# HGRN output products split into score and state parts, chunk-state and inverse products in turn over row groups

## What is computed

```python
# HGRN2, per head and chunk of 64 tokens (q, k, v: tokens x 128)
inter  = (q * exp(b)) @ S                       # what the state gives
scores = sum_k q[t,k] * k[s,k] * exp(b[t,k] - b[s,k]), s <= t
o      = inter + scores @ v
S      = exp(b_end) * S + (k * exp(b_end - b)).T @ v

# gated delta rule: per head and chunk T = inverse(I + A), A strictly lower triangular 64 x 64
```

## Time and profile before

| | |
|---|---|
| Runs, median of 3 | 2732.92 us (2729.94 to 2734.82) |
| Profiled execution, span from first to last instruction | 2725.5 us |
| its own time outside of the span | not recorded; the median of the runs is 7.4 us above the span |
| Mean granted TensorE clock | 0.995 of 2.4 GHz |
| Busy: TensorE, its weight loads, VectorE, ScalarE, GpSimd | 98%, 65%, 46%, 24%, 2% |
| Load of a 2 MB weight block, issue to landing, median | 7.8 us |

### The profile page before, as it was taken

How to read it: one execution, slowest core, us unless ns; L and a number is a source line. 1 busy time by engine, 2 the same in 40 slices (tenths; PEclk the granted TensorE clock), 3 DMA queues, 4 the chain that set the end, 5 groups by cost and what they waited for, 6 DMA issues and landing times.

```text
span 2725.5 us, 28695 instructions
## 1 busy us (share of the span) xinstructions
PE 2672.6 (98%) x11362; PEld 1773.7 (65%) x11362; DVE 1259.9 (46%) x2490; ACT 658.4 (24%) x1491; POOL 60.1 (2%) x116
## 2 busy tenths in 40 slices
PE   8999999999999999999999999999999999999999
PEld 4445557656478888746556664655555684788886
DVE  5733333444334456425363426465564451344564
ACT  2122331246200000222342123525252202000001
POOL 0000000000000000000000001011010000000000
PEclk9999999999999999999999999999999999999999
DMA  4211012100122222120110131121120411222222
GB/s 156 76 48 62 31 64 82 61 32 10 66 80 93 93 93 70 69 93 32 62 62 32 64 124 55 39 78 47 62 76 34 177 62 62 92 93 93 81 74 78
DMA packets 120445, 194.88 MB, mean 71 GB/s; under 512 B 5148, under 2 KB 61272, under 8 KB 119416
## 3 DMA queue, kind: packets, MB, share of 16 engines
q1 hardware_dynamic: 118848, 180.82, 19.6%
q0 software_dynamic: 1344, 12.19, 1.2%
q10 hardware_dynamic: 120, 0.03, 0.0%
HBM read 185.69 MB, written 7.34 MB: 71 GB/s over the span
## 4 chain that ended last, share of the span: by engine, by line
PE 96%; ACT 2%; DVE 1%; issue 1%; DMA 0%; ACTq 0%; DVEq 0%
PE psum L532 20%; PE psum L529 15%; PE psum L2312 14%; PE psum L418 9%; PE psum L2294 8%; PE psum L403 6%; PE psum L438 5%; PE psum L1165 2%; PE psum L2162 2%; PE psum L455 2%; PE psum L1185 2%; PE psum L462 1%; PE psum L1173 1%; PE psum L660 1%; PE psum L391 1%
## 5 line engine op out<-in xcount | busy, mean ns | idle before, releaser
L2312 PE MATMUL psum<-weight_ring,h_t 128*128 128x512 f32 x896 | 409.0, 600 | 3.1 <-ACT arena L2593 1.9
L585 DVE TENSOR_TENSOR arena<-arena,psum 128x512 f32<-128x512 f32 x179 | 122.9, 687 | 346.7 <-PE psum L532 287.6
L2312 PEld LDWEIGHTS psum<-weight_ring,h_t 128*128 128x128 f32 x896 | 163.3, 192 | 165.8 <-issue 162.4
L418 PE MATMUL psum<-h_t,weight_ring 128*128 128x512 f32 x544 | 235.6, 594 | 2.2 <-DVEq L3032 0.8
L2294 PE MATMUL psum<-h_t,weight_ring 128*128 128x512 f32 x512 | 233.0, 598 | 0.9 <-DVE arena L2912 0.9
L532 PE MATMUL psum<-h_t,weight_ring 128*128 128x256 f32 x1024 | 228.2, 380 | 0.0
L529 PE MATMUL psum<-weight_ring,arena 128*128 128x256 f32 x992 | 222.2, 382 | 2.3 <-ACT arena L2722 1.5
L532 PEld LDWEIGHTS psum<-h_t,weight_ring 128*128 128x128 f32 x1024 | 194.9, 190 | 27.1 <-issue 1.3
L529 PEld LDWEIGHTS psum<-weight_ring,arena 128*128 128x128 f32 x992 | 189.9, 192 | 28.8 <-issue 3.3
L418 PEld LDWEIGHTS psum<-h_t,weight_ring 128*128 128x128 f32 x544 | 102.9, 190 | 130.9 <-issue 128.9
L403 PE MATMUL psum<-weight_ring,h_t 128*128 128x512 f32 (+1 forms) x384 | 162.3, 580 | 0.8 <-DVEq L1640 0.8
(11 more groups left out here) (409 smaller groups left out, 3407.6 us busy)
## 6 DMA issues: line engine op xcount, KB each, us to landing
weight_ring<-in_ffn_w_in_dram SPq DMA_DIRECT2D x44, 1024.0 KB, 6.8
weight_ring<-in_w_in_dram SPq DMA_DIRECT2D x20, 2048.0 KB, 7.8
weight_ring<-in_ffn_w_out_dram SPq DMA_DIRECT2D x8, 2048.0 KB, 7.9
weight_ring<-in_w_in_even_dram SPq DMA_DIRECT2D x7, 2048.0 KB, 8.2
weight_ring<-in_w_in_odd_dram SPq DMA_DIRECT2D x5, 2048.0 KB, 7.8
weight_ring<-in_w_in_dram SPq DMA_DIRECT2D x8, 1024.0 KB, 7.0
weight_ring<-in_w_branch_gdn_dram SPq DMA_DIRECT2D x4, 2048.0 KB, 7.8
weight_ring<-in_ffn_w_out_dram SPq DMA_DIRECT2D x4, 1536.0 KB, 6.9
```

The source lines that it names most:

```text
L418: last = pe.matmul(bank, slot[:, k, c:c + P], act[:, k, :], start=(k == 0), stop=(k == KD - 1))
L585: ins = dve.tensor_tensor(out, other, bank, op)
L2312: last = pe.matmul(bank, act[:, k, t * P:(t + 1) * P], slot[:, k, :], start=(k == 0), stop=(k == KD - 1))
```

## The change

In `pe_hgrn_states` the chunk-state products alternate between the two row halves with every product instead of filling one bank and then the other. The outputs are split: the score products of all four tiles go first, into banks of their own (`hd`), ahead of the wait for the states; then the state products of all four tiles, into four banks `ho`, which no longer accumulate. ScalarE copies `hd`, scaled, to `V["o"]`; VectorE adds `ho`, scaled, to it, and ScalarE's squares wait for that. In `pe_gdn_inverse_and_state` the `x5` products alternate between the two halves, and `t5`, `r5` of half 1 and `r5` of half 0 take turns unit by unit.

```diff
--- before.py
+++ after.py
@@ -2259,24 +2259,29 @@
         pe.wait_ge(K.free_of((s, "ke", g, h)), K.turn((s, "ke", g, h)))
         if h == 3:
             pe_take(fill, KD)
-        for par in range(2):
-            p = CH * par
-            bank = pe_fresh(K, pe, (s, "hu", g, h, par))
-            for j in range(NT):
-                last = pe.matmul(bank[:, j * P:(j + 1) * P], V["k"][p:p + CH, h, j * P:(j + 1) * P],
-                                 V["v"][p:p + CH, j, h * P:(h + 1) * P], start=True, stop=True)
-            last.then_inc(K.full_of((s, "hu", g, h, par)), 1)
+        banks = [pe_fresh(K, pe, (s, "hu", g, h, par)) for par in range(2)]
+        for j in range(NT):
+            for par in range(2):
+                p = CH * par
+                ins = pe.matmul(banks[par][:, j * P:(j + 1) * P], V["k"][p:p + CH, h, j * P:(j + 1) * P],
+                                V["v"][p:p + CH, j, h * P:(h + 1) * P], start=True, stop=True)
+                if j == NT - 1:
+                    ins.then_inc(K.full_of((s, "hu", g, h, par)), 1)
     pe_take(fill, KD)
+    for j in range(NT):
+        bank = pe_fresh(K, pe, (s, "hd", g, j))
+        for h in range(4):
+            last = pe.matmul(bank[:, h * P:(h + 1) * P], V["s_t"][:, h * NT + j, :], V["v"][:, j, h * P:(h + 1) * P],
+                             start=True, stop=True)
+        last.then_inc(K.full_of((s, "hd", g, j)), 1)
     pe.wait_ge(K.hgrn_states, g + 1)
     for j in range(NT):
         bank = pe_fresh(K, pe, (s, "ho", g, j))
         for h in range(4):
-            o = bank[:, h * P:(h + 1) * P]
-            last = pe.matmul(o, V["s_t"][:, h * NT + j, :], V["v"][:, j, h * P:(h + 1) * P], start=True, stop=False)
             for c in (2 * j, 2 * j + 1):
                 p = CH * (c % 2)
-                last = pe.matmul(o[p:p + CH, :], V["w"][:, 0, h * T + c * CH:h * T + (c + 1) * CH],
-                                 V["state"][:, h * NC + c, :], start=False, stop=True)
+                last = pe.matmul(bank[p:p + CH, h * P:(h + 1) * P], V["w"][:, 0, h * T + c * CH:h * T + (c + 1) * CH],
+                                 V["state"][:, h * NC + c, :], start=True, stop=True)
         last.then_inc(K.full_of((s, "ho", g, j)), 1)
     K.banks_in_turn = ALL_BANKS
 
@@ -2420,27 +2425,29 @@
     lower, rr, tt, x5, x6 = V["lower"], V["rr"], V["tt"], V["x5"], V["x6"]
     units = range(4 * NT)
     pe.wait_ge(K.blocks_solved, 2 * g + 1)
-    for p in range(2):
-        bank = pe_fresh(K, pe, (s, "x5", g, p))
-        a, b = slice(64 * p, 64 * p + 32), slice(64 * p + 32, 64 * p + 64)
-        for u in units:
-            last = pe.matmul(bank[b, 32 * u:32 * u + 32], lower[a, u, b], V["block"][a, u, :], start=True, stop=True)
-        last.then_inc(K.full_of((s, "x5", g, p)), 1)
+    banks = [pe_fresh(K, pe, (s, "x5", g, p)) for p in range(2)]
+    for u in units:
+        for p in range(2):
+            a, b = slice(64 * p, 64 * p + 32), slice(64 * p + 32, 64 * p + 64)
+            ins = pe.matmul(banks[p][b, 32 * u:32 * u + 32], lower[a, u, b], V["block"][a, u, :], start=True, stop=True)
+            if u == units[-1]:
+                ins.then_inc(K.full_of((s, "x5", g, p)), 1)
     pe_take(fill, 4)
     pe.wait_ge(K.blocks_solved, 2 * g + 2)
     for p in range(2):
         pe.wait_ge(K.free_of((s, "x5", g, p)), K.turn((s, "x5", g, p)))
     b = slice(32, 64)
-    bank = pe_fresh(K, pe, (s, "t5", g))
+    turned = pe_fresh(K, pe, (s, "t5", g))
+    banks = [pe_fresh(K, pe, (s, "r5", g, p)) for p in range(2)]
     for u in units:
-        last = pe.matmul(bank[b, 32 * u:32 * u + 32], V["block_t"][b, u, :], x5[b, u, :], start=True, stop=True)
-    last.then_inc(K.full_of((s, "t5", g)), 1)
-    for p in range(2):
-        a, b = slice(64 * p, 64 * p + 32), slice(64 * p + 32, 64 * p + 64)
-        bank = pe_fresh(K, pe, (s, "r5", g, p))
-        for u in units:
-            last = pe.matmul(bank[a, 32 * u:32 * u + 32], x5[b, u, :], V["block_t"][b, u, :], start=True, stop=True)
-        last.then_inc(K.full_of((s, "r5", g, p)), 1)
+        ins = pe.matmul(turned[b, 32 * u:32 * u + 32], V["block_t"][b, u, :], x5[b, u, :], start=True, stop=True)
+        if u == units[-1]:
+            ins.then_inc(K.full_of((s, "t5", g)), 1)
+        for p in (1, 0):
+            a, c = slice(64 * p, 64 * p + 32), slice(64 * p + 32, 64 * p + 64)
+            ins = pe.matmul(banks[p][a, 32 * u:32 * u + 32], x5[c, u, :], V["block_t"][c, u, :], start=True, stop=True)
+            if u == units[-1]:
+                ins.then_inc(K.full_of((s, "r5", g, p)), 1)
     pe_take(fill, 4)
     pe.wait_ge(K.blocks_placed, 6 * g + 2)
     pe.wait_ge(K.free_of((s, "t5", g)), K.turn((s, "t5", g)))
@@ -2575,9 +2582,11 @@
         else:
             act_gate(K, act, V["gate_y"], (s, "gate_h", 0), 0)
         for j in range(NT):
+            act.wait_ge(K.full_of((s, "hd", g, j)), K.turn((s, "hd", g, j)))
+            act.activation(V["o"][:, j, g * 512:(g + 1) * 512], K.bank((s, "hd", g, j)), ACT.Copy,
+                           scale=DK ** -0.5).then_inc(K.free_of((s, "hd", g, j)), 1)
+        for j in range(NT):
             dst = V["o"][:, j, g * 512:(g + 1) * 512]
-            act.wait_ge(K.full_of((s, "ho", g, j)), K.turn((s, "ho", g, j)))
-            act.activation(dst, K.bank((s, "ho", g, j)), ACT.Copy, scale=DK ** -0.5).then_inc(K.free_of((s, "ho", g, j)), 1)
             act.wait_ge(K.free_of((s, "ho", g, j)), K.turn((s, "ho", g, j)))
             for h in range(4):
                 n = j * 4 + h
@@ -2959,6 +2968,12 @@
                         key = (s, "hu", g, h, c % 2)
                         dve.wait_ge(K.free_of(key), K.turn(key))
         dve.tensor_copy(K.stat[:, 76:77], K.stat[:, 77:78]).then_inc(K.hgrn_states, 1)
+        for j in range(NT):
+            o = V["o"][:, j, g * 512:(g + 1) * 512]
+            dve.wait_ge(K.free_of((s, "hd", g, j)), K.turn((s, "hd", g, j)))
+            dve.wait_ge(K.full_of((s, "ho", g, j)), K.turn((s, "ho", g, j)))
+            dve.scalar_tensor_tensor(o, K.bank((s, "ho", g, j)), DK ** -0.5, o, ALU.mult, ALU.add).then_inc(
+                K.free_of((s, "ho", g, j)), 1)
         dve_head_norm(K, dve, V["o"], g * 512, 128, V["gate"], K.hgrn_squares, g + 1,
                       K.hgrn_gated)
         dve.drain().then_inc(K.phase_met, 1)
```

## The result

The changed kernel takes 2705.8 us (median of four executions, 2704.7 to 2708.9). The kernel before, measured beside it, gave 2729.9, 2732.9 and 2734.8; a fourth execution of 4014.4 us, whose cause is not known, is left out of the comparison. The ratio is 0.9904, with a 95% interval of 0.9893 to 0.9916. 2709.3 was forecast. The profiled execution took 2706.6 us, its span is 2704.9; so some 1.8 us lie around a span, not the 7.4 that the median seemed to be above it in the kernel before.

What follows compares the result with a forecast made beforehand. TensorE was taken as the bound, by how densely it issues. Outputs 10.6, chunk states 3.2, inverse 8.8 and clock 1.0 sum to 23.6 us; 2732.9 less that gives 2709.3. Own range 2705 to 2713; 8 in 10: 2704 to 2719.

Steps and rivals of the forecast that it cites:

- the 7.4: Gap between the profiled span, 2725.5 us, and the median of the runs, 2732.9; taken as unchanged by the change.
- What bounds the kernel: Whole kernel: TensorE, busy for 98% of the span, pays for what it issues; the question is how densely.
- Outputs: Output products, twice: 12.83 us per group becomes 7.6 with fewer shape changes and paired narrow products; saves 10.6 in all.
- Chunk states: Chunk-state products, twice: 3.93 and 1.71 us become 2.9 and 1.1 by pairing row halves; saves 3.2 in all.
- The formula from L1460: Chunk states: 0.1 at the entry, 0.11 per further pair, 0.27 drain; gives 0.70 for L1460's 8 instructions, seen at 0.72.
- Inverse: Inverse products, four times: x5 1.15 us, saving 0.9; t5 with both r5 1.66, saving 1.3; 8.8 in all.
- the bound that I kept for the range: In t5 with both r5: three tiles at once would take 1.15 us and save 1.8, 2.0 more in all.
- The rival of 2719: Instruction supply keeps only today's pace beyond 16 queued matmuls, so the inverse saves nothing: 2719.1 us; chance 0.14.
- Alternation costs a drain: Chunk states and inverse: each row-group change costs 0.1 us, 38 against 10.6 saved, so slower: 2760; chance 0.03.
- The tail: After the outputs, squares end 1.0 us later, within 2.6 of slack; rival: it shows, 1 us per group, 2711.3; chance 0.06.
- The clock: TensorE's low-clock stretch of 3.41 us behind the third group's t5 and r5: 1.0 us saved, between nothing and 1.66.

Runs made afterwards that it cites:

- runs of 384: The changed kernel with the whole turn of t5 and both r5 issued four times over, 384 instructions per group: 2755.9 us.
- runs of 192 at one tile at a time: The kernel before with t5 and each r5 issued twice over, 192 instead of 96 instructions per group: 2756.2 us.

## Why the prediction was right, and where it was off

**What bounds the kernel.** Right. On TensorE nothing but the order and density of the instructions was changed, no new wait came, and the 24.4 us read from the places stand against 25.7 and 23.8 of clock-free span.

**Outputs.** Forecast 7.6 per group, measured 7.65; 10.6 against 10.4. The wide run took 3.67 to the next shape (forecast 3.6), the narrow 3.71 (3.7). The small difference is one change of shape: the prediction itself read 0.35 for two of them in the old order, 0.175 each, but priced the one behind the wide run by the transposes' 0.1, which is another change (128x128 to 64x128). 0.17 was right. 64 narrow products in 3.71 keep the pairs of the earlier trace rows over the whole length. Alone it gave 10 to 11 us at equal clock.

**Chunk states.** Forecast 2.9 and 1.1, measured 2.95 and 1.16, 3.2 against 3.1. The formula from L1460 held.

**Inverse.** This is the term that was mis-sized: "t5 with both r5 takes 96 x 0.0158 + 0.14 = 1.66 and saves 1.3". It took 1.13 and saved 1.82, since three tiles worked at once; this was the bound that I kept for the range, 2.0 us in all, and should have been the value. The three products of one unit lie on three different 32x32 tiles, and what the trace of before showed was two tiles at 0.0158, each of them still at 0.0305. The order in pairs shows that directly: with `t5` by itself and the two `r5` in pairs, 64 of the 96 at 0.016, the same products took 2.05. `x5` came as forecast, 1.13 for 1.15.

**Supply.** The rival of 2719 is refuted for this change: 96 products ran at 0.0107 without a stop. The lead of 16 matmuls in the earlier trace rows spoke for that, and rightly, but it could not show the other limit: a block of 256 instructions that is used up before the next is there. Runs of 96 stay clear of it, since no block fits into 192 instructions. The page TensorE: Matmul & The Clock Gate of the Trainium skill, section "Wait — 56ns, not 53.3ns?", has starts at least about 25 ns apart. Within one tile this case's 30.5 ns agree; over three tiles the trace has 10.7 on average, so it disagrees.

**Alternation costs a drain.** Refuted: alternating row groups were faster in each single run. What costs is another tile *shape*: 0.17 per change between 128x128 and 128x64.

**The tail.** It got longer as forecast and reached nothing. VectorE's additions (L2975) take 0.69 each, the squares of the last tile end 2.7 us behind TensorE's part. In the second group, the last addition and the gating on VectorE, then the gates on ScalarE:

```profile
1487.21 0.69 DVE L2975 SCALAR_TENSOR_TENSOR arena<-psum,arena 128x512 f32<-128x512 f32 x1 [0.18 <-PE psum L2283]
...
1496.37 2.87 DVE L3064 TENSOR_TENSOR arena<-arena 128x512 f32<-128x512 f32 x4
```

```profile
1499.32 0.60 ACT L2649 ACTIVATE arena<-psum 128x512 f32<-128x512 f32 x1 [3.44 <-DVEq L2979]
1501.42 0.60 ACT L2649 ACTIVATE arena<-psum 128x512 f32<-128x512 f32 x1 [1.51 <-PE psum L2317]
```

The first gate now waits for the gating (3.44), but the second still waits for TensorE's own product for 1.51, where it was 2.51 in the earlier trace rows. The forecast 1.0 of the 2.6 us of slack was used, 1.5 are left.

**The clock, and the 7.4 us.** Here two things were taken too simply. I counted 1.0 for the clock, from the stretch behind the third delta group. It did go, in every profile with the new order, and with it the 1.66 that it cost. But the stretches elsewhere come and go between executions by more than that: the first profile after has more low clock in all than the one before (17.0 lost against 11.9), the second less (10.2). And I took the 7.4 us between span and median as lying around the span and therefore unchanged. They are about 1.8 around it; the rest is clock: the profiled execution had a mean of 0.995, and 2732.9 is the time of executions at 0.993. Neither error moved the forecast much, because the medians compared are both of executions at 0.993 to 0.994.

The account in numbers: the forecast was 22.6 without the clock, and the places show 24.4; 2.1 more came from the third tile, 0.3 less from the rest. At an equal rounded clock the kernels are 24.1 to 26.1 us apart (for instance 2730.6 and 2704.8 at 0.994). Between the medians it was 27.1 in the first measurement and 22.6 in the second. So of the 3.5 us by which 2705.8 lies below the forecast, 1.8 were mis-sized in the places, and the rest is which executions fell into the median; that part of the closeness is luck.

## What to carry to other kernels

Small matmuls of different tiles run side by side if they stand next to each other in the program; so ask of every run of equal small products how many tiles it could use in turn, and group what remains by shape. Count tiles, not pairs, when you price it: one slot holds as many products as there are different tiles, up to four here. Keep a dense run below 256 instructions, loads counted, so that no whole block of the instruction stream lies in it; a longer one may pass or stop, by where it lies. And compare single-digit gains in microseconds at equal clock, or part by part in the timeline: two real gains of about 3 us did not show in medians of 11 runs.

## What the runs showed of the hardware that I had not expected

- Three 32x32 tiles take 96 fp32 products in 1.13 us, 0.0107 each with a weight load before every one; four 128x32 tiles take 64 in 1.88.
- TensorE can stand still for 0.7 to 4.6 us in the middle of an unbroken run without any wait in the program, at places that don't move with the pace: the stops are whole multiples of 256 TensorE instructions apart (256 to 1792; one count of nine is 1537 instead of 1536), and come only behind a block that lay wholly in the run. The DMA list shows the block for each: a packet of 16384 bytes on an instruction queue, which lands 1.2 to 1.5 us before TensorE goes on.
- From block to block it took 3.5 to 4.0 us with idle DMA engines and up to 6.2 with a weight block on them.
- In the four runs of 384 the granted clock fell to 0.50 during the first stop or within 1 us behind it, for 10.2 to 13.7 us. It also fell in all four runs of 192 at one tile at a time, 4.6 to 5.8 us after their start, two of them without any stop. In and behind the dense run of 96 it was 1.00 in all four groups.
- A change between the 128x128 and the 128x64 shape costs 0.17 us, with 31 changes in a stretch as with 7.
